# A two-block transformer kernel: small steps held back in TensorE's order, pool groups in a lane of their own, the second output projection's rows dealt out anew

## What is computed

```python
h = rms_norm(x, ln1)                                   # first block
qkv_a, beta_a, decay_a, z_a, qkv_b, gate_a, gate_b = split_columns(h @ w_in)
y_a = gated_deltanet(qkv_a, beta_a, decay_a, z_a, ...) @ w_branch_a   # 8 heads, chunks of 64
y_b = moba_attention(rope(q_b), rope(k_b), v_b) @ w_branch_b          # 8 heads
x = x + (sigmoid(gate_a) * y_a + sigmoid(gate_b) * y_b) @ w_out
u_gate, u_val = split(causal_dwconv(rms_norm(x, ln2) @ w_up))
x = rms_norm(x + (silu(u_gate) * u_val) @ w_down, final_norm)

h = rms_norm(x, attn_norm_2)                           # second block
z = h @ w_in_2                                         # 1024 pool columns, 3 * 1024 + 288 shifted
d = causal_multiscale_pool(z_pool)                     # windows 2, 4, 8, 16 over 4 groups of 256
pool_out = einsum('btgc,gcd->btgd', d, pool_w) * pool_scale
rwkv_out = rwkv7_time_mix(token_shift(z_rest), ...)    # 16 heads of 64, a recurrence over time
x = x + concatenate([pool_out, rwkv_out]) @ w_out_2    # rows 0-1023 pool, 1024-2047 rwkv
x = x + relu(rms_norm(x) @ w_ffn_up_2) ** 2 @ w_ffn_down_2
x = x + sigmoid(rms_norm(x) @ w_ple_gate_2) * (p @ w_ple_proj_2)
return rms_norm(x, final_norm_2)
```

## Time and profile before

| | us |
|---|---|
| median of 3 runs (lowest, highest) | 2874.83 (2873.76, 2877.68) |
| the profiled execution | 2877.99 |
| its span | 2876.2 |
| PE busy in the span | 2794.6 (97%) |
| DVE busy | 1896.2 (66%) |
| ACT busy | 1495.7 (52%) |
| mean granted clock of TensorE | 0.991 |

### The profile page before, as it was taken

The page is one execution under the profiler, slowest core; times in us unless marked ns, Lnnn a source line. Parts: engine busy times, 40 slices in busy tenths (PEclk is TensorE's granted clock), DMA queues, the critical chain, the costliest instruction groups (busy, mean ns, idle before and its releaser), DMA issues.

```text
span 2876.2 us, 40656 instructions
## 1 busy us (share of the span) xinstructions
PE 2794.6 (97%) x16324; PEld 2443.5 (85%) x16324; DVE 1896.2 (66%) x2237; ACT 1495.7 (52%) x2026; POOL 154.8 (5%) x131
## 2 busy tenths in 40 slices
PE   8998999999999999999999998989999999999998
PEld 7988987888888888888888997978888888888886
DVE  6467766545668777777777676666766666666665
ACT  5456655444455455455546565555544444444464
POOL 0010111000000000000000022110000000000000
PEclk9999999999999999999999999999999999999999
DMA  5544522655555655655565531212555555555544
GB/s 215 191 149 134 175 89 89 196 193 187 185 197 184 195 193 190 191 190 184 191 194 177 184 124 70 99 35 102 200 190 191 188 193 192 187 196 191 191 169 161
DMA packets 133820, 485.47 MB, mean 169 GB/s; under 512 B 14944, under 2 KB 16352, under 8 KB 133120
## 3 DMA queue, kind: packets, MB, share of 16 engines
q1 hardware_dynamic: 133632, 482.87, 50.1%
HBM read 480.71 MB, written 2.10 MB: 168 GB/s over the span
## 4 chain that ended last, share of the span: by engine, by line
PE 84%; DVE 7%; ACT 5%; issue 3%; DMA 1%; POOL 0%; DVEq 0%; ACTq 0%; SPq 0%; POOLq 0%
PE psm L193 77%; PE psb L193 6%; ACT ar L209 2%; DVE ar L231 2%; DVE ar L221 1%; PE psb L196 1%; DMA raw<-in_w_in 1%; DVE slo L221 1%; ACT shi L209 1%; DVE gs L231 0%; ACT L209 0%; DVE x L221 0%; ACT gs L209 0%; POOL ar L221 0%; ACT hf L209 0%
## 5 line engine op out<-in xcount | busy, mean ns | idle before, releaser
L221 DVE TENSOR_TENSOR slo<-raw,shi 128x1024 fp32r<-128x1024 f32 (+1 forms) x901 | 1117.0, 1244 | 624.9 <-ACT shi L209 622.8
L209 ACT ACTIVATE shi<-raw 128x1024 fp32r<-128x1024 f32 (+1 forms) x901 | 946.5, 1053 | 1026.7 <-PE psm L193 864.9
L193 PE MATMUL psm<-shi,gs 128*128 128x512 f32 x2016 | 638.0, 392 | 0.0
L193 PE MATMUL psm<-hs,shi 128*128 128x512 f32 (+1 forms) x2528 | 563.7, 346 | 0.0
L193 PE MATMUL psm<-gs,shi 128*128 128x256 f32 (+2 forms) x2592 | 552.0, 330 | 10.7 <-DVE slo L221 9.9
L193 PEld LDWEIGHTS psm<-gs,shi 128*128 128x128 f32 (+1 forms) x2592 | 432.2, 191 | 50.4 <-DVE slo L221 10.5
L193 PEld LDWEIGHTS psm<-hs,shi 128*128 128x128 f32 x2528 | 427.0, 189 | 47.7 <-issue 0.8
L193 PE MATMUL psm<-shi,hs 128*128 128x512 f32 x1408 | 445.8, 392 | 3.7 <-DVE hs L221 2.7
L193 PEld LDWEIGHTS psm<-shi,gs 128*128 128x128 f32 x2016 | 379.4, 188 | 78.8 <-issue 1.2
L193 PE MATMUL psm<-slo,gs 128*128 128x512 f32 x1008 | 393.2, 390 | 0.0
L193 PE MATMUL psm<-gs,slo 128*128 128x256 f32 (+1 forms) x1808 | 366.9, 284 | 0.0
(11 more groups left out here) (185 smaller groups left out, 1646.4 us busy)
## 6 DMA issues: line engine op xcount, KB each, us to landing
raw<-in_w_in SPq DMA_DIRECT2D x240, 512.0 KB, 3.6
raw<-in_w_up SPq DMA_DIRECT2D x176, 512.0 KB, 4.2
raw<-in_w_ffn_up SPq DMA_DIRECT2D x128, 512.0 KB, 4.2
raw<-in_w_ffn_down SPq DMA_DIRECT2D x128, 512.0 KB, 4.3
raw<-in_w_down SPq DMA_DIRECT2D x88, 512.0 KB, 3.7
raw<-in_w_out SPq DMA_DIRECT2D x64, 512.0 KB, 3.6
raw<-in_w_ple_gate SPq DMA_DIRECT2D x32, 512.0 KB, 4.0
raw<-in_w_branch_b SPq DMA_DIRECT2D x16, 512.0 KB, 4.3
```

The costliest lines, as they stand in the source:

```text
L193: return self.issued(self.eng and self.eng.matmul(out, lhs, rhs, start=start, stop=stop, skip_group_check=True), cost)
L209: return self.issued(self.eng and self.eng.activation(out, in_, fn, scale=scale, **kw), cost)
L221: return self.issued(self.eng and self.eng.tensor_tensor(out, a, b, op), self.cost(out))
```

## The change

1. A slack. `ready` hands out a step only when its due time plus `slack[0]` has passed. The slack is 1.5 us (of the planner's account) from the start until all groups of branch_a are in the order, 0.0 through out and the first FFN, 0.4 from lora on, and 0.0 again ahead of out2b(3). Forced steps know no slack.
2. A fifth lane. Pool groups 2g + 1 stand in a lane of their own beside 2g, and each of the two has its own small scan buffer.
3. Rows of w_out_2. out2a takes 4 tiles, rows 0 and 256 (pool groups 0, 1), then 1024 and 1280 (rw 0 to 3); out2b(2) takes 3, rows 512 and 768 (pool groups 2, 3) and 1536 (rw 4, 5); out2b(3) takes row 1792 as before. The same 8 tiles for each f. The events are now awaited tile by tile also in out2b, and TensorE waits for each 128-row piece.

```diff
-        plan.append((("out2a", f), [("w_out_2", row + 256 * i, 2, 512 * f, 512) for row in (1024, 0, 512) for i in range(2)]))
+        plan.append((("out2a", f), [("w_out_2", row, 2, 512 * f, 512) for row in (0, 256, 1024, 1280)]))
     for h in (2, 3):
         for f in range(4):
-            group(("out2b", h, f), "w_out_2", 1024 + 256 * h, 512 * f, 512, 2)
+            plan.append((("out2b", h, f), [("w_out_2", row, 2, 512 * f, 512) for row in ((512, 768, 1536) if h == 2 else (1792,))]))
...
             if kind == "out2a":
-                return ((lambda k: (hs, 8 + k) if k < 4 else (gs, k - 4)),
-                        (lambda k: ("rw", k) if k < 4 else ("pl", (k - 4) // 2)), ())
+                return (lambda k: (gs, k) if k < 4 else (hs, 4 + k)), (lambda k: ("pl", k // 2) if k < 4 else ("rw", k - 4)), ()
+            if kind == "out2b" and name[1] == 2:
+                return (lambda k: (gs, 4 + k) if k < 4 else (hs, 8 + k)), (lambda k: ("pl", 2 + k // 2) if k < 4 else ("rw", k)), ()
             if kind == "out2b":
-                return lambda k: (hs, 8 + 2 * name[1] + k), None, [("rw", c) for c in (2 * name[1], 2 * name[1] + 1)]
+                return (lambda k: (hs, 14 + k)), (lambda k: ("rw", 6 + k)), ()
...
-        pc = two(gf[:, 7936:7968])
+        pcs = [two(gf[:, 7936 + 32 * i:7968 + 32 * i]) for i in range(2)]
...
-                pd = two(gf[:, 1024 * wi:1024 * wi + 512])
+                pd, pc = two(gf[:, 1024 * wi:1024 * wi + 512]), pcs[wi % 2]
...
-            order, lanes, want, first = [], [[], [], [], []], [[], [], [], []], []
-            low, building, pairs, whole, held = [], [0], [], [], []
+            order, lanes, want, first = [], [[], [], [], [], []], [[], [], [], [], []], []
+            low, building, pairs, whole, held, slack = [], [0], [], [], [], [1.5]
...
-                return [w for w in range(4) if lanes[w] and all(known(c) for c in want[w])]
+                return [w for w in range(5) if lanes[w] and all(known(c) for c in want[w])]
...
-                while ws := [w for w in open_lanes() if due(w) <= max(pe.t, until)]:
+                while ws := [w for w in open_lanes() if due(w) + slack[0] <= max(pe.t, until)]:
...
-                    lanes[2] += [drive(("pool", 2 * name[1])), drive(("pool", 2 * name[1] + 1))]
+                    lanes[2].append(drive(("pool", 2 * name[1])))
+                    lanes[4].append(drive(("pool", 2 * name[1] + 1)))
...
-                    if part and (norm_of.get(kind_of(name)) or name[0] in ("out", "out2a")):
+                    if part and (norm_of.get(kind_of(name)) or name[0] in ("out", "out2a", "out2b")):
...
                 group(("branch_a", g))
+            slack[0] = 0.0
             build_norm(1)
...
             advance("open_second")
+            slack[0] = 0.4
             group(("lora", 0))
...
-                until((dve_step, ("rw", 2 * h)), (dve_step, ("rw", 2 * h + 1)))
                 if h == 3:
                     until(lambda: not any(lanes))
                     build_norm(3)
+                    slack[0] = 0.0
                 for f in range(4):
                     group(("out2b", h, f))
```

## The result

The changed kernel takes 2892.22 us (median, 2889.66 to 2893.59) against 2875.69 us before (2873.76 to 2877.68). The ratio is 1.0052, with a 95% interval of 1.0040 to 1.0064, so it is slower by 12 to 18 us. The forecast was 2870 us in 2857 to 2884: the sign and the range were both wrong.

What follows compares the result with a forecast made beforehand. TensorE, busy 2794.6 of 2876.2 us, was taken as the bound, with only 81.6 us of idle time to win. Terms −11.5 + 2 + 6.8 − 2.5 = −5.2 us from the median 2874.83 gave 2870 us, range 2857 to 2884.

Steps and rivals of the forecast that it cites:

- D: Second recurrence, 0.4 us slack: about ten short waits up to 1850 get shorter, −2.5 us, bounds 0 and −6.
- the 10 to 12 that I had named as the sign: Second recurrence, windows of the pairs before the drain: 10 to 12 us of idle time in sum.
- C: Recurrence tail: filler used up, last six steps in a row and out2b(3) waits; +6.8 us, bounds 0 and +12.
- R2: Second recurrence's end: filler spent early, out2b(3) waits for rw 7, outweighing the first block's gain; +9, 2884 us; chance 0.20.
- B: Drain ahead of output projection: two pool tiles come first, their scans may delay the chain; +2 us, bounds −6 and +8.
- A: First block, 1.5 us slack: filler covers attention and delta chain waits, saves a clock fall; −11.5 us, bounds −3 and −20.
- R3: Whole kernel: lateness moves along, held-back steps delay ScalarE and VectorE followers and the next step waits; 2875 us; chance 0.18.
- E: The rest: second scan buffer, fifth lane, tiles, DMAs and their splitting cost nothing.

Runs made afterwards that it cites:

- e2: Kernel before with only the 0.4 us slack in the second recurrence, lora to out2b(3): ratio 1.0058, +17 us.
- e5: Changed kernel with 0.0 in place of the 0.4 us slack from lora on, all other parts kept: ratio 0.9999 against the kernel before, 0 us.
- e6: Kernel before with 0.4 us slack from lora to the end of pool(1) only: ratio 1.0034, +10 us.
- e3: Kernel before with only the fifth lane for pool groups and the two small scan buffers: ratio 1.0011, +3 us.
- e1: Kernel before with only the 1.5 us slack in the first block, up to the last branch_a group: ratio 1.0007, +2 us.
- e17: Kernel before with only the held gives (copies of pairs 0 to 2 into hs) in a lane of their own: ratio 0.9989, −3 us.
- e4: Kernel before with only w_out_2's rows dealt anew and the tile-by-tile waits belonging to it: ratio 0.9995, −1 us.
- e13: e6 plus a drain rule counting pair 3's lane as due 3 us later until its give is out: ratio 1.0052 against the kernel before, +15 us.
- e8: Kernel before with a slack of −0.4 us (steps handed over early) from lora to out2b(3): ratio 1.0058, +17 us.
- e12: Kernel before with a slack of 0.1 us from lora to out2b(3): ratio 1.0016, +5 us.
- e9: Kernel before with 0.4 us slack beside the lora and rkv groups only: ratio 1.0034, +10 us.
- e10: Kernel before with 0.4 us slack beside pool(0) and pool(1) only: ratio 1.0041, +12 us.
- e16: Kernel before with w_out_2's rows dealt anew and the held gives in a lane of their own: ratio 0.9968, −9 us.
- e15: Changed kernel without the 0.4 us slack, with the held gives in a lane of their own: ratio 0.9982 against the kernel before, −5 us.

## Why the prediction was wrong, by its own steps

- **D, the step that failed.** I took each held-back step of the second recurrence as a wait shortened, −2.5 us, 0 to −6, and gave it no loss side at all. Measured it is +17 us (e2), and the changed kernel without it is as fast as before (e5). Its waits up to 1850 did get a little shorter (11.3 us idle for 13.2, with the 10 to 12 that I had named as the sign); what I left out is that the recurrence has little filler ahead of a point where its results are wanted, and that a step held back while filler lasts is handed over later where none is left. e6 shows it: 0.4 us beside lora, rkv and the pool groups only, and 9.9 us more idle time in the drain. I had written this for the tail ("each later step is held back by 0.4 us more") but priced it there alone, and the lower clock of such rows at 1.5 us.
- **C**, +6.8: right in place and mechanism, the returns right within 0.1 us, too small by the 2.04 us wait ahead of them and by the clock. Idle time in 2011:2090 grew by 6.0 us, and the clock of 0.91 is 79 × 0.09 = 7 us more. It needs the slack: e5 has the same rows and no such tail. The rival R2, at 0.20, is this mechanism, and its +16 for the second block is close to what came (with the first block's saving missing); but it made them from the rows and the lane with D at nothing, and these two without the slack measure 0 (e5), so that its size is a coincidence.
- **B**, +2: idle time in 1850:1910 grew by 4.9 us, within my bounds −6 to +8; the clock there fell from 0.91 to 0.80, which I had not counted. It too is mainly the slack's: the rows alone measure −1, the lane alone +3. The lane's +3 has the sign that I gave it, but not the place: e3 is idle for 11.8 us in 1850:1910 (13.3 before) and for 5.7 in 1910:2011 (2.3 before). VectorE time put ahead of the pairs in the drain is not shown.
- **A**, −11.5: measured +2, interval −1 to +5. The traces say the same: the last transposes of the norm ahead of lora stand at 1561.7 us in the mean of the five with this slack and at 1562.0 in the other fifteen, which lie between 1560.3 and 1564.2. R3 described it: lateness moves along. The waits of transposes turned into waits of filler for slo and into fewer but longer ones in the delta chain, and the clock of 330:500 fell from 0.99 to 0.97 (0.97 in e1 too, though e3 and e17 have that without this slack). My reasoning that work that fills the gap "isn't new" left out that the engines behind the step are given their share later as well; I read this from the waits, no run isolates it.
- **E**, the tiles and DMAs at nothing: no sign against it, the rows alone (e4) measure −4 to +1.
- R3, at 0.18, was right for the first block; for the whole, at 2875 us, it wasn't. The rule of the Trainium skill ("TensorE: Matmul & The Clock Gate", section "Architectural detail: the array is 16× 32×32") that ScalarE and VectorE are strictly in order is seen in the drain, where ScalarE stood for 6.82 us ahead of one copy with pair 4's behind it; e13 shows that this wait alone is not the price.

What stays open: why −0.4 us costs 17 us as well. Its idle time in 1757:2062 is only 3.7 us above before and its clock the same. Between the two norms e8 and e12 have

```profile
1562.18:2082.65 520.47, 482.21 (x3550) 434.88 (x3550) 339.37 (x525) 293.00 (x538) 62.76 (x75) 0.98 0.35 114
```

```profile
1563.42:2072.71 509.29, 480.21 (x3545) 437.08 (x3545) 337.65 (x525) 290.18 (x538) 68.02 (x75) 0.96 0.35 116
```

e8 is 14.9 us longer there, with 7.8 us more idle time: more in 1660:1760 (8.8 us for 3.0) and in 1910:2011 (15.4 for 2.3), less in the drain, which is nearly closed (2.7 for 13.3). The other 7.1 us are busy time at a clock of 0.98, no lower than the 0.97 of before: more busy time for the same matmuls is not always the clock's. A rival also stays: that the order of before is a lucky one and nearly any other handing out of the pairs' steps costs 10 us or more. For it are e8, the halves that don't add up (e9, e10, e6) and e13. Against it are e16, e15 and e5, other orders that are as fast or faster, and that adding the 0.4 us to the first two or the last costs 20, 17 and 15 us again. And the split of the slack's cost into idle time and clock is read from windows; no run changed the one without the other.

## What to carry to other kernels

A rule that delays steps to spare an in-order engine a short wait must be priced at the next point where the chain's result is awaited with no filler left: here the loss came back there, together with TensorE's lower clock, and it didn't follow the size of the delay (5, 17 and 15 us for 0.1, 0.4 and 0.8). Look first for what stands in a list ahead of an awaited result without being needed for it: taking the gives from behind two pool groups and dealing the rows so that these groups are wanted later is one line and a table, and gave 0.32% where tuning the slack in either direction lost. And test the parts of such a change one by one: three were near nothing, one made the whole loss.

## What the runs showed of the hardware

A kernel can be slower with less idle time: e12 had 24.6 us of idle time against 26.9 and was 5 us slower, at a granted clock of 0.93 against 0.96 over 305 us; between the two norms, with the same work, it had 29.1 us of idle time against 30.5 and was 3.7 us longer. In the tail of the changed kernel TensorE was busy for 0.51 of the 2 us of 2044:2046 and for 1.06 of those of 2046:2048, at 1.00 and 0.97; then the clock fell, and in 2048:2056, small matmuls with waits of 0.4 us between them, it stayed at 0.50 although TensorE was busy for 6.77 of 8 us. The same steps took 1.7 to 2 times as long there as at full clock.
